# One block product fewer in the last MLP chunk of a hybrid decoder block: seven products for its first half, and the last outputs added up in the products' own banks

## The reference

```python
h2 = rmsnorm(x, g_mlp[l])
u = jax.nn.relu(jnp.einsum('bsd,df->bsf', h2, w_ff1[l]))     # 256 x 1024 by 1024 x 4096
x = x + jnp.einsum('bsf,fd->bsd', u * u, w_ff2[l])           # 256 x 4096 by 4096 x 1024
return rmsnorm(x, g_final)
```

## Time and profile before

| | us |
|---|---|
| median of 3 runs | 360.95 |
| lowest, highest | 360.7, 361.22 |
| the profiled execution | 361.16 |
| its span, first to last instruction | 359.4 |
| PE busy in it | 353.2 |
| DVE, ACT, POOL busy | 286.0, 229.2, 39.7 |

### The profile page before, as it was taken

How to read it: one execution, slowest core, us unless ns; L and a number is a source line. 1 busy time by engine, 2 the same in 40 slices (tenths; PEclk the granted TensorE clock), 3 DMA queues, 4 the chain that set the end, 5 groups by cost and what they waited for, 6 DMA issues and landing times.

```text
span 359.4 us, 5546 instructions
## 1 busy us (share of the span) xinstructions
PE 353.2 (98%) x2119; PEld 311.3 (87%) x2119; DVE 286.0 (80%) x402; ACT 229.2 (64%) x371; POOL 39.7 (11%) x61
## 2 busy tenths in 40 slices
PE   8999999999999999999999999999999999999994
PEld 8998889988888888888888999999999999999983
DVE  3878971789968747496687879999998898998585
ACT  4996445899675743182566567777668777665424
POOL 1242000000001000000022021111110111310001
PEclk9999999999999999999999999999999999999999
DMA  7998667491637245148076999999999999953003
GB/s 259 378 392 281 266 183 236 153 350 74 235 111 229 83 163 176 60 156 310 3 233 171 321 299 231 266 297 307 293 274 263 259 259 267 319 154 117 2 0 117
DMA packets 42197, 76.77 MB, mean 214 GB/s; under 512 B 1923, under 2 KB 19344, under 8 KB 41920
## 3 DMA queue, kind: packets, MB, share of 16 engines
q1 hardware_dynamic: 37840, 66.59, 53.8%
q0 software_dynamic: 4176, 9.64, 13.5%
q10 hardware_dynamic: 160, 0.27, 0.2%
HBM read 75.44 MB, written 1.05 MB: 213 GB/s over the span
## 4 chain that ended last, share of the span: by engine, by line
PE 98%; POOLq 0%; DVE 0%; issue 0%; DVEq 0%; ACT 0%; POOL 0%
PE ps L1455 30%; PE ps L1456 29%; PE ps L1457 29%; PE ps L1462 4%; PE ps L1677 2%; PE ps L1704 2%; PE ps L1562 1%; PE ps L1571 1%; PE ps L1600 0%; PE ps L1595 0%; PE ps L1605 0%; POOLq L130 0%; DVE qkT_b L1446 0%; DVEq L130 0%; ACT prob L586 0%
## 5 line engine op out<-in xcount | busy, mean ns | idle before, releaser
L566 ACT ACTIVATE whi<-raw 128x1024 fp32r<-128x1024 f32 (+3 forms) x127 | 118.8, 989 | 18.0 <-PE ps L1457 17.4
L964 DVE TENSOR_TENSOR wlo<-raw,whi 128x1024 fp32r<-128x1024 f32 (+1 forms) x56 | 64.0, 1186 | 14.9 <-ACT whi L566 14.9
L1455 PE MATMUL ps<-whi,xT_hi 128*128 128x512 f32 (+2 forms) x188 | 72.6, 386 | 0.0
L1457 PE MATMUL ps<-whi,xT_lo 128*128 128x512 f32 (+2 forms) x188 | 71.2, 379 | 0.0
L1456 PE MATMUL ps<-wlo,xT_hi 128*128 128x512 f32 (+2 forms) x188 | 71.1, 378 | 0.0
L1457 PE MATMUL ps<-xT_hi,wlo 128*128 128x256 f32 x224 | 63.4, 283 | 0.0
L1456 PE MATMUL ps<-xT_lo,whi 128*128 128x256 f32 x224 | 63.4, 283 | 0.0
L1455 PE MATMUL ps<-xT_hi,whi 128*128 128x256 f32 x224 | 63.3, 283 | 0.0
L1455 PE MATMUL ps<-whi,lat_hi 128*128 128x512 f32 (+1 forms) x124 | 47.6, 384 | 0.0
L1456 PE MATMUL ps<-wlo,lat_hi 128*128 128x512 f32 (+1 forms) x124 | 47.3, 382 | 0.0
L1457 PE MATMUL ps<-whi,lat_lo 128*128 128x512 f32 (+1 forms) x124 | 47.2, 381 | 0.0
(11 more groups left out here) (165 smaller groups left out, 524.5 us busy)
## 6 DMA issues: line engine op xcount, KB each, us to landing
raw<-in_w_ff_dram SPq DMA_DIRECT2D x32, 1024.0 KB, 6.8
raw<-in_w_in_dram SPq DMA_DIRECT2D x14, 1024.0 KB, 6.3
raw<-in_w_out_dram SPq DMA_DIRECT2D x4, 1024.0 KB, 5.0
t_raw<-in_w_ff_dram SPq DMA_DIRECT2D x12, 256.0 KB, 7.7
raw<-in_w_ff_dram POOLq DMA_DIRECT2D x12, 256.0 KB, 4.8
t_raw<-in_w_ff_dram POOLq DMA_DIRECT2D x12, 256.0 KB, 7.1
gates<-in_b_gate_dram POOLq DMA_DIRECT2D x2, 1024.0 KB, 7.9
raw<-in_w_o_a_dram SPq DMA_DIRECT2D x2, 1024.0 KB, 5.2
```

Source lines behind the costliest of these rows:

```text
L566: return nc.scalar.activation(dst, src, ACT.Copy, scale=scale)
L964: nc.vector.tensor_tensor(wlo[:, s, h * w:(h + 1) * w], raw[:, s, h * w:(h + 1) * w], whi[:, s, h * w:(h + 1) * w].bitcast(F32), ALU.subtr ...
L1455: nc.tensor.matmul(dst, a_hi, b_hi, start=start, stop=False, skip_group_check=on_sums)
L1457: return nc.tensor.matmul(dst, a_lo, b_hi, start=False, stop=stop, skip_group_check=on_sums)
```

## The change

- `LAST_PRODUCTS`, `mlp_products_last`: half 0 of chunk 7 is also done by seven block products, in the order P1, P6, P5, P7, P2, P3, P4. The four that are only read raise `last_products`. For this DVE's and ACT's loops take in chunk 6, so that `block_sums`, `low_w2`, `left_sums`, `high_t24`, `high_t3` and so on run for (7,0); SP loads the block for T3 too, and POOL issues `sum_blocks(FAST, 0)`.
- Half 1 of chunk 7 stays plain, but its three first outputs accumulate onto banks P2, P3 and P4 (`OUT_BANK`) instead of fresh ones, and the last output's two parts onto what DVE has written into P5's and P1's bank (`pre_add`, `TAIL_BANK`). S4 changes its sign so that P3 can be added. Its weights go into slot 0 instead of slot 3, its hidden values into `xT_hi` and `xT_lo`.
- On PE, the second half of `mlp_products(6, 1)` (five products) is moved behind `mlp_in` of (7,1), which so comes five block products sooner.
- `combine_banks` shrinks from seven instructions to four; of `combine_rows` the parts 0 and 1 stand ahead of `residual(0)`, part 2 between `residual(0)` and `gain(0)`.

```diff
+LAST_PRODUCTS = tuple(PRODUCTS[i] for i in (0, 5, 3, 2, 4, 6, 1))
+OUT_BANK = (P2, P3, P4)
+TAIL_BANK = (P5, P1)
...
-                if 1 <= c < FAST:
+                if c:
                     sp.dma_start(t3_raw[:, p, :], w2_rows(c, p)[:, 0, HALF:D]).then_inc(t3_landed[p], 16)
...
-            load_w2(FAST, 1)
+            sp.wait_ge(w1_lo, 4 * FAST - 2)
+            sp.dma_start(ff_slot(0).rearrange("p (f n) -> p f n", f=2),
+                         w2_rows(FAST, 1)).then_inc(raw_landed[U_FF % SLOTS], 16)
...
             pool.tensor_scalar(g_fin_row, g_fin_row, ROOT_D, None, ALU.mult).then_inc(gfin_ready, 1)
+            sum_blocks(FAST, 0)
...
-            with act.Fori(2, FAST - 1) as c:
+            with act.Fori(2, FAST) as c:
                 mlp_chunk(c)
-            mlp_chunk(FAST - 1, last=True)
-            u_high(0)
-            act.wait_ge(w2_used, 2 * FAST)
+            lefts_high(FAST, 0)
+            high_last()
+            relu_square(FAST, 1)
+            u_high()
+            act.wait_ge(last_products, 1)
             copy(p1_copy, ps[:, P1, :]).then_inc(p1_read, 1)
-            high_last(1)
-            relu_square(FAST, 1)
-            u_high(1)
...
+            def pre_add():
+                dve.wait_ge(bank_read, 4)
+                for n in range(2):
+                    cols = slice(n * QUART, (n + 1) * QUART)
+                    nc.vector.tensor_tensor(tail[n], xs[:, 1, HALF + n * QUART:HALF + (n + 1) * QUART],
+                                            q_sum[:, cols], ALU.add).then_inc(pre_added, 1)
...
-            mlp_chunk(FAST - 1, last=True)
-            u_low(0)
+            left_sums(FAST, 0)
+            lefts_low(FAST, 0)
+            low_last(0)
+            low_last(1)
+            u_low()
             combine_banks()
-            low_last(1)
-            u_low(1)
-            combine_rows()
+            pre_add()
+            combine_rows(0)
+            combine_rows(1)
...
             dve.wait_ge(gfin_ready, 1)
-            residual(0, ff_done, fin_res)
+            dve.wait_ge(comb_part, 1)
+            residual(0, ff_done, fin_res, OUT_BANK)
+            combine_rows(2)
             gain(0)
-            residual(1, ff_done, fin_res)
+            dve.wait_ge(comb_part, 2)
+            residual(1, ff_done, fin_res, OUT_BANK)
             gain(1)
...
-            mlp_chunk(FAST - 1, end=True)
+            mlp_in_unit(FAST - 1, 1)
+            mlp_products(FAST - 1, 0)
+            mlp_in_unit(FAST, 0)
+            mlp_products(FAST - 1, 1, part=slice(0, 2))
             mlp_in_unit(FAST, 1)
+            mlp_products(FAST - 1, 1, part=slice(2, 7))
+            mlp_products_last()
             pe.wait_ge(last_lo, 2)
             pe.wait_ge(uT_lo_done, 3)
-            mlp_out_last(0, 0, 0)
-            mlp_out_last(0, 0, 1)
-            mlp_out_last(1, 0, 0)
-            pe.wait_ge(last_lo, 4)
-            pe.wait_ge(uT_lo_done, 4)
-            mlp_out_last(0, 1, 0)
-            mlp_out_last(0, 1, 1)
-            mlp_out_last(1, 0, 1)
-            mlp_out_last(1, 1, 0)
-            mlp_out_last(1, 1, 1)
+            mlp_out_last(P2, 0, 0, HALF)
+            mlp_out_last(P3, 0, HALF, HALF)
+            mlp_out_last(P4, 1, 0, HALF)
+            pe.wait_ge(pre_added, 2)
+            mlp_out_last(TAIL_BANK[0], 1, HALF, QUART)
+            mlp_out_last(TAIL_BANK[1], 1, HALF + QUART, QUART)
```

More of the change, by code:

```diff
@@ L193, in hybrid_block @@
         left_raw = [rows[:, 2 * p:2 * p + 2, :].rearrange("p a b -> p (a b)") for p in range(2)]
-        tail_bank = ps[:, U_BANK, P:P + QUART]
+        tail = [ps[:, bank, 0:QUART] for bank in TAIL_BANK]
+        u_last_hi, u_last_lo = (h[:, 0:2, :].rearrange("p a b -> p (a b)") for h in (xT_hi, xT_lo))
         p1_copy, v_sum, q_sum = t3_raw[:, 0, :], t3_raw[:, 1, :], t24_raw[:, 0, :]
@@ L874, in lefts_high, with u_high, mlp_chunk @@
                 copy(left_hi_of[p][:, 0:LEFTS], left_raw[p][:, 0:LEFTS]).then_inc(left_hi, 1)
[L876 to L881, removed]
+            def u_high():
+                act.wait_ge(u_sq, 2 * FAST + 2)
+                copy(u_last_hi, left_raw[1][:, HALF:]).then_inc(uT_hi_done, 1)
+            def mlp_chunk(c, first=False):
                 if first:
@@ L893, in mlp_chunk @@
                 lefts_high(c, 1)
[L894 to L901, removed]
+                high_blocks(c + 1, 0)
+                high_t24(c + 1, 0)
+                relu_square(c + 1, 0)
+                high_t3(c + 1, 0)
             relu(0, 0)
@@ L944, in _ @@
             act.wait_ge(ff_done, 4)
[L945 removed]
+            squares(tail[0], QUART, SSQ_FIN + 3, prob[:, 3, 0:QUART])
             act.wait_ge(ff_done, 5)
[L947 removed]
+            squares(tail[1], QUART, SSQ_FIN + 4, prob[:, 3, QUART:HALF])
             final_act(0, 1)
@@ L1203, in _, with residual @@
             turned_low(3, mT_hi, mT_lo, 1, 1, 0.5)
-            def residual(i, done, ready):
+            def residual(i, done, ready, banks=ROW_BANK):
                 t, n = divmod(i, 2)
@@ L1208, in residual @@
                 xr = xs[:, t, n * HALF:(n + 1) * HALF]
-                nc.vector.tensor_tensor(xr, ps[:, ROW_BANK[i], :], xr, ALU.add).then_inc(ready, 1)
+                nc.vector.tensor_tensor(xr, ps[:, banks[i], :], xr, ALU.add).then_inc(ready, 1)
             def h_norm(t):
@@ L1282, in low_w2, with low_last @@
                 low_sums(p, c * 8 + 4 * p - 6)
[L1284 to L1290, removed]
+            def low_last(h):
+                s, w = U_FF % SLOTS, SLOT_W // 2
+                dve.wait_ge(last_hi, h + 1)
+                nc.vector.tensor_tensor(wlo[:, s, h * w:(h + 1) * w], raw[:, s, h * w:(h + 1) * w],
+                                        whi[:, s, h * w:(h + 1) * w].bitcast(F32), ALU.subtract).then_inc(last_lo, 1)
             def left_sums(c, p):
@@ L1337, in combine_banks @@
-                nc.vector.tensor_tensor(c21, ps[:, P4, :], c21, ALU.add).then_inc(bank_read, 1)
-                dve.wait_ge(bank_read, 5)
-                nc.vector.tensor_tensor(c21, ps[:, P7, :], c21, ALU.add).then_inc(bank_read, 1)
+                dve.wait_ge(last_products, 4)
                 nc.vector.scalar_tensor_tensor(out=c22, in0=ps[:, P7, :], scalar=-1.0, in1=c22, op0=ALU.mult,
                                                op1=ALU.add).then_inc(bank_read, 1)
[L1343 to L1350, removed]
+                nc.vector.tensor_tensor(c21, ps[:, P7, :], c21, ALU.add).then_inc(bank_read, 1)
@@ new lines, in pre_add, with combine_rows @@
+            def pre_add():
[4 more added lines that the diff above has]
+                                            q_sum[:, cols], ALU.add).then_inc(pre_added, 1)
+            def combine_rows(i):
+                part, op = ((p1_copy, ALU.add), (q_sum, ALU.add), (v_sum, ALU.subtract))[i]
+                c = xs[:, i // 2, i % 2 * HALF:(i % 2 + 1) * HALF]
+                nc.vector.tensor_tensor(c, c, part, op).then_inc(comb_part, 1)
@@ L1357, in square, with mlp_chunk @@
                     .then_inc(u_sq, 1)
-            def mlp_chunk(c, first=False, last=False):
+            def mlp_chunk(c, first=False):
                 left_sums(c, 0)
@@ L1374, in mlp_chunk @@
                 low_w1(c + 1, 1, (1,))
[L1375 to L1379, removed]
+                block_sums(c + 1, 0)
+                low_w2(c + 1, 0)
             def u_rows_low(t):
@@ L1426, in _ @@
                                            op1=ALU.add).then_inc(fin_sum, 1)
[L1427 to L1431, removed]
+            dve.wait_ge(comb_part, 3)
+            residual(2, ff_done, fin_res, OUT_BANK)
             dve.wait_ge(fin_res, 3)
@@ L1443, in _ @@
             dve.wait_ge(fin_rstd, 2)
-            for n, src in enumerate((ps[:, ROW_BANK[3], 0:QUART], tail_bank)):
+            for n, src in enumerate(tail):
                 cols = slice(HALF + n * QUART, HALF + (n + 1) * QUART)
@@ L1814, in mlp_out_rows, with mlp_out_last @@
                 return m
[L1816 to L1837, removed]
+            def mlp_out_last(bank, t, start, width):
+                for f in range(2):
+                    w = slice(f * D + start, f * D + start + width)
+                    b = ((A11, A21), (A12, A22))[f][t] - A11
+                    a = slice(b * P, (b + 1) * P)
+                    m = product(ps[:, bank, 0:width], u_last_hi[:, a], u_last_lo[:, a], whi[:, U_FF % SLOTS, w],
+                                wlo[:, U_FF % SLOTS, w], False, f == 1, bank in TAIL_BANK)
+                m.then_inc(ff_done, 1)
             def mlp_in_unit(c, p):
@@ L1843, in mlp_in_unit, with block_product @@
                 mlp_in(p).then_inc(u_done, 1)
-            def mlp_products(c, p, first=False, end=False):
-                s = (U_FF + 2 + p) % SLOTS
-                pe.wait_ge(left_lo, c * 2 + p - 1)
-                pe.wait_ge(w2_lo, c * 8 + 4 * p - 4)
-                for bank, a, b in PRODUCTS:
+            def block_product(p, bank, a, b, start=False, stop=False):
```

(29 more changed lines are left out.)

41 lines of the change are left out of this document (15 added, 26 removed).

## The result

The changed kernel takes 361.53 us (median of 17 runs, 361.07 to 361.99); the kernel before, timed beside it, 360.86 (17 runs, 360.52 to 361.22). The ratio is 1.0019, with a 95% interval of 1.0012 to 1.0026: slower by 0.67 us. That is under the 0.2% that the prediction took for the least a measurement can tell, but with 17 runs of each the interval is 0.07% to either side, so the loss is clear of noise. Forecast were 361.4 and +0.48 us, in a range of 360.5 to 362.1. The profiled execution took 361.43 us with a span of 359.6.

The account below looks back on a forecast made before the run. PE was taken to bound the kernel, with rows 0's chain 0.21 us behind; PE would end 0.68 us sooner, but that chain would end the kernel later: 360.95 + 0.48 = 361.43, rounded 361.4, range 360.5 to 362.1.

Parts of the forecast that it names:

- PE's part: Matmuls on PE: 5.46 us of plain outputs removed, 4.78 us of block products added, net -0.68 us.
- The supply of (7,0): Loads and sums feeding chunk (7,0): arrive in time, cost 0; PE stalls only if the T1 sum lands after 330.7.
- DVE between 343 and 349: DVE's steps from v_sum to combine_rows 1: free at 349.2, 0.2 us ahead of residual(0); pre_add causes no stall.
- moving five products changes no count: PE, products of (6,1) put behind mlp_in of (7,1): same matmuls in another order up to 342.98 us.
- The chain over rows 0: DVE, POOL and ACT at the end: residual(1) at 351.20, +1.11 us; ACT's last accumulator +0.48 us.
- POOL's two steps ... follow as before.: Kernel's end, behind ACT's last accumulator: POOL's two steps, DVE's last scaling and the stores follow unchanged.
- The step of 0.61 us: Independent DVE instructions start 0.61 us apart, dependent ones 0.73; the skill's rule would make three steps 0.36 us longer.
- rival 2: DVE's added steps cost 0.73 us each, delaying residual(0) or residual(1): 361.8 us; chance 0.10.
- Rival 1: PE's saving arrives at the kernel's end, not held by DVE's or ACT's order: 360.27 us; chance 0.08.
- rival 3: T1 sum of (7,0) lands behind 330.7 and PE stalls at mlp_in of (7,1): 361.7 to 362.9 us; chance 0.12.
- What bounded the kernel before: PE, busy 353.2 of 359.4 us, with a second chain over rows 0 beside it having 0.21 us to spare.

Follow-up runs that it names:

- the late sum above: Changed kernel with 24 chained POOL memsets ahead of the accumulating DMAs of (7,0), so its T1 sum lands later: 367.87 us, 1.0197.
- the last pair: Both kernels without DVE's squares over rows 1's first half and one store, the changed also with ACT's last squares first: 360.54 us (0.9990); before 361.15 us (1.0003).
- POOL's help: Changed kernel with ACT's last squares ahead of final_act(0, 0) and combine_rows(2) given to POOL: 360.85 us, 1.0004.
- that version: Changed kernel with ACT's last squares ahead of final_act(0, 0) and DVE's sum of squares over rows 1's first half left out: 360.88 us, 1.0002.

## Why the prediction was right, point by point

- **PE's part.** Right: the seven products took 4.76 us, forecast 4.78, PE ended 0.7 us sooner, nothing stalled.
- **The supply of (7,0).** Right: POOL issued at 322.34, ACT copied both halves of the weights in one go from 326.55 (2.00 us) without waiting for the sum, and the late sum above puts the cover where the prediction had it.
- **DVE between 343 and 349.** Right in its sum: after, DVE was idle for 0.14 us ahead of `residual(0)`, forecast 0.2. But "moving five products changes no count" was only half of that step. Undone, it costs 0.85 us, by way of ACT's order; the prediction had read the move on PE alone.
- **The chain over rows 0.** Right in mechanism and nearly in size: `residual(1)` at 18.79 us behind the anchor, forecast 351.20 - 332.44 = 18.76; the last accumulator +0.46, forecast +0.48. Moving the step away, and moving ACT's squares, each shorten the kernel.
- **"POOL's two steps ... follow as before."** This failed. The sum held no term for POOL waiting on DVE. The add was held by the scaling of rows 1, which DVE itself could start only behind ACT's first accumulator: +0.20 us. 0.46 + 0.20 = 0.66, the measured 0.67. The trace before had it to be seen, though none of its rows that I had picked out shows it: DVE's scaling ran until 354.95, and POOL's add, from 354.80, ended 0.06 us behind it.

```profile
354.27 0.68 DVE L1441 TENSOR_TENSOR qkT_b<-xs,qkT_b 128x512 f32<-128x512 f32 x1
```
- **The step of 0.61 us.** `residual(0)` to `residual(1)` took 1.81 us after, three steps of 0.60 and not of 0.73, and DVE was idle ahead of `residual(0)`: with that rival 2 falls. The prediction had put the 3 x 0.73 us beside a rule of the Trainium skill ("VectorE: DVE Perf Modes", "The DRAIN you can't avoid"). It had read the rule too strictly: the section adds that a next instruction which isn't held starts earlier, and that agrees with the steps of 0.60; that a semaphore costs nothing extra doesn't, as a step with a wait takes 0.72 here. Rival 1 would have needed three things gone at once, as the last pair shows; rival 3 needed 3.9 us.
- **What bounded the kernel before.** I named one near chain with 0.21 us to spare. There were two: the kernel before, with one more add, stalled PE itself at `pre_add`, which had 0.07 us to spare.

Still open: no version tried that computes the whole output is below the kernel before. The squares first, with or without POOL's help, bring the changed kernel level with it (1.0005 and 1.0004). A version in which the stores start early and ACT's squares don't wait either wasn't tried.

## What to carry to other kernels

When PE is 98% busy, its end isn't the kernel's end: write down for each engine's chain behind the last outputs how much time it has to spare (here 0.07 for `pre_add`, 0.21 for ACT's order, and then the stores). A saving on PE is worth no more than the smallest of those that the change leaves in place, and what then ends last is the next engine's order. An instruction added on DVE is paid for where its chain has nothing to spare: here 0.47 us and not its step of 0.60, as it also filled the 0.12 us of a wait. And where DVE reads two SBUF operands, look at what POOL does in that moment.

## What the runs showed of the hardware

- POOL and a DVE instruction with two SBUF operands hold each other where both read SBUF. An add of one column on POOL took 0.19 us alone, 0.41 beside a DVE product of two SBUF operands and 0.57 where that had only begun, ending 0.04 to 0.06 us behind it each time; the inverse root 0.88 instead of 0.56; and the other way round a DVE product took 1.14 instead of 0.69. The Trainium skill ("SBUF — State Buffer", section "Who interferes with whom") says just that: a DVE instruction with two SBUF inputs contends with a GpSimd instruction that reads SBUF. These traces agree.
- After 5.2 us without work PE's granted clock was 0.50 (1.2 GHz), and back at 1.00 (2.4 GHz) after some 4 us of matmuls without a gap (338.33 to about 342.7 in that trace), which added 2.0 us to the stall.
- Five output stores of 1 MB together took from 355.0 to 357.8 us, at up to 393 GB/s, and were the last bound of that version: with one store less the end came some 0.25 us sooner from the anchor, with D unchanged.
